# The per-layer embedding's projection issued in one piece ahead of the sum of squares

## The reference

```python
def rms_norm(x, g):
    xf = x.astype(jnp.float32)
    y = xf * lax.rsqrt(jnp.mean(xf * xf, axis=-1, keepdims=True) + EPS)
    return (y * g.astype(jnp.float32)).astype(x.dtype)

def per_layer_embed(h, p_i, g, w_gate, w_proj):
    gate = jax.nn.sigmoid((rms_norm(h, g) @ w_gate).astype(jnp.float32))
    return h + (gate * (p_i @ w_proj).astype(jnp.float32)).astype(h.dtype)

# first block
        x = x + moe(rmsnorm(x, g_ffn[i]), ...)
        gate = jax.nn.sigmoid(jnp.einsum('bsd,de->bse', rmsnorm(x, g_ple[i]), w_ple_gate[i]))
        x = x + jnp.einsum('bsp,pd->bsd', p[i], w_ple_proj[i]) * gate
# second block, for each of two layers
        h = h + peer_ffn(rms_norm(h, norm_ffn[i]), ...)
        h = per_layer_embed(h, p[i], norm_ple[i], ple_w_gate[i], ple_w_proj[i])
```

## Time and profile before

| | us |
|---|---|
| median of 3 runs | 3065.58 (3065.04 to 3068.65) |
| the profiled execution | 3064.01 |
| its span, first to last instruction | 3062.2 |
| TensorE busy | 2637.0 (86%) |
| VectorE busy | 1343.3 (44%) |
| mean granted clock of TensorE | 0.937 |
| first, second, third embedding: start of the projection | 1159.5, 2048.4, 3006.0 |

### The profile page before, as it was taken

One profiled execution on the slowest core, in us unless ns is written; L12 is line 12 of the kernel. 1 busy time (PEld: TensorE's weight loads), 2 busy tenths in 40 slices (PEclk: granted clock), 3 DMA queues, 4 the chain that ended last, 5 costly groups with the idle time before them and its releaser, 6 DMA issues.

```text
span 3062.2 us, 29257 instructions
## 1 busy us (share of the span) xinstructions
PE 2637.0 (86%) x10044; PEld 1391.2 (45%) x10044; DVE 1343.3 (44%) x3484; ACT 544.5 (18%) x1283; POOL 509.5 (17%) x556
## 2 busy tenths in 40 slices
PE   8789999999999998997778777789888778787787
PEld 6554444444443436784333333347677333333335
DVE  2222221212212223416777777641234777777752
ACT  0210010000101002202222222211331222122212
POOL 1000000000000000004333333300012333333320
PEclk9779999999999998998998999999889898989999
DMA  6259999999999993349999999953216999999990
GB/s 216 94 208 417 417 419 417 418 417 418 418 417 419 417 406 113 128 137 393 421 421 422 421 421 421 421 231 123 90 61 256 422 421 421 422 421 422 421 420 34
DMA packets 169837, 1025.92 MB, mean 335 GB/s; under 512 B 17488, under 2 KB 17904, under 8 KB 71184
## 3 DMA queue, kind: packets, MB, share of 16 engines
q0 software_dynamic: 74880, 540.05, 42.5%
q1 hardware_dynamic: 94864, 484.73, 40.1%
HBM read 1022.09 MB, written 2.62 MB: 335 GB/s over the span
## 4 chain that ended last, share of the span: by engine, by line
PE 44%; DMA 36%; DVE 8%; SPq 7%; issue 2%; ACT 2%; POOL 1%; DVEq 0%; ACTq 0%; POOLq 0%
DMA big<-in_uv,small 28%; PE ps L424 12%; PE ps L569 11%; PE ps L739 9%; DMA big<-in_w_gate_up 7%; SPq L342 4%; PE ps L559 3%; SPq L334 2%; PE ps L604 1%; DVE big L1477 1%; PE ps L414 1%; PE ps L437 1%; POOL big L1587 1%; PE ps L683 1%; DMA big<-in_w_down 1%
## 5 line engine op out<-in xcount | busy, mean ns | idle before, releaser
L739 PE MATMUL ps<-big,small 128*128 128x512 f32 x2048 | 1008.1, 650 | 283.8 <-ACT small L1039 283.8
L1587 POOL DMA_INDIRECT big<-in_uv,small x512 | 484.1, 946 | 2174.4 <-DVE small L1466 1406.6
L739 PEld LDWEIGHTS ps<-big,small 128*128 128x128 f32 x2048 | 415.2, 208 | 872.7 <-issue 492.9
L1477 DVE SCALAR_TENSOR_TENSOR big<-big,ps 128x1024 f32<-128x1024 f32 x512 | 617.6, 1219 | 349.6 <-DMA big<-in_uv,small 347.9
L569 PE MATMUL ps<-big 128*64 128x512 f32 x3072 | 705.8, 600 | 24.2 <-DMA big<-in_w_gate_up 21.6
L569 PEld LDWEIGHTS ps<-big 128*64 128x64 f32 x3072 | 202.9, 137 | 421.6 <-issue 333.9
L424 PE MATMUL ps<-hT,ring 128*128 128x256 f32 x1408 | 317.4, 388 | 14.5 <-DVE hT L1126 11.5
L424 PEld LDWEIGHTS ps<-hT,ring 128*128 128x128 f32 x1408 | 272.9, 195 | 58.6 <-DVE hT L1126 13.1
L1039 ACT ACTIVATE small<-con,small 128x128 f32<-128x128 f32 x512 | 163.6, 390 | 293.1 <-DVE small L1484 293.1
L1303 DVE COPY big<-ps 128x512 f32<-128x512 f32 x32 | 22.1, 692 | 426.1 <-PE ps L569 426.1
L1289 DVE TENSOR_TENSOR big<-ps,big 128x256 f32<-128x256 f32 x64 | 27.2, 425 | 308.2 <-PE ps L586 308.2
(11 more groups left out here) (246 smaller groups left out, 1633.2 us busy)
## 6 DMA issues: line engine op xcount, KB each, us to landing
big<-in_w_gate_up SPq DMA_DIRECT2D x256, 1024.0 KB, 20.5
big<-in_w_down SPq DMA_DIRECT2D x128, 1024.0 KB, 24.2
ring<-in_peer_w_q SPq DMA_DIRECT2D x32, 512.0 KB, 3.7
ring<-in_w_in SPq DMA_DIRECT2D x16, 512.0 KB, 5.2
ring<-in_a_w_in SPq DMA_DIRECT2D x16, 512.0 KB, 3.6
ring<-in_ple_w_gate SPq DMA_DIRECT2D x16, 512.0 KB, 5.9
big<-in_uv,small POOLq DMA_INDIRECT x512, 26.3
ring<-in_w_kv SPq DMA_DIRECT2D x16, 512.0 KB, 3.7
```

The costliest lines, as they stand in the source:

```text
L739: last = pe.matmul(ps[:, out_bank(tt) + z, :], diagonal(k), rows(k)[:, D + z * BANK:D + (z + 1) * BANK], start=(k % (PH * PTOP) == 0), sto ...
L1477: ins = dve.scalar_tensor_tensor(u, u, 1.0, tok, op0=ALU.mult, op1=ALU.mult, accum_out=dots[:, k:k + 1])
L1587: pool.indirect_dma_start(out=rows(k), out_offset=None, in_=io[f"uv{L}"], in_offset=bass.IndirectOffsetOnAxis(ap=rows_at[:, k:k + 1], axis ...
```

## The change

The projection's two halves are issued one behind the other, and `sum_squares` follows them. The wait for the residual is moved behind the projection, directly ahead of `sum_squares`. It can't be dropped, since `sum_squares` writes bank 7, which VectorE reads while it adds. The projection's banks 0 to 3 are not read by the adds. The number of instructions stays the same on every engine, and only TensorE's order changes, in all three places.

```diff
             def ple(k, norm, reads):
 
-                pe.wait_ge(x_ready, 4 * (norm - 1) + 4)
                 n = first[f"proj{k}"]
                 pe.wait_ge(p_loaded, 16 * (k + 1))
                 for c in range(2):
@@ -683,8 +682,8 @@
                         last = pe.matmul(half(0, e), w[:, e * P:(e + 1) * P], tile(pT, c),
                                          start=(c == 0 and e % 2 == 0), stop=(c == 1), skip_group_check=True)
                     last.then_inc(w_used, 1)
-                    if c == 0:
-                        sum_squares(norm)
+                pe.wait_ge(x_ready, 4 * (norm - 1) + 4)
+                sum_squares(norm)
                 dense(first[f"ple{k}"], hsrc, 4, h_ready, DT * reads)
```

## The result

The changed kernel takes 3079.09 us (median of 10 executions, 3072.27 to 3086.68), the kernel before 3067.77 us (10 executions beside them, 3064.95 to 3072.42). The ratio is 1.0036, 95% interval 1.0025 to 1.0048: 11 us slower, 8 to 15 by the interval. The profiled execution took 3076.04 us with a span of 3074.2, against 3064.01 and 3062.2.

What follows compares the result with a forecast made beforehand. TensorE's own work was taken to set the time in all three places. Stage 1 at +3.15 + 1.65, stages 2 and 3 at +3.15 - 0.97 + 1.65 each, gave +12.4 on 3065.6: 3078.0 us, range 3071 to 3083.

Steps and rivals of the forecast that it cites:

- The uncovered norm: Sum of squares to gate product, each stage: without the half between, 3.46 + 6.60 replaces 6.91 us, +3.15 per stage.
- The earlier start: Second and third stage: the projection no longer waits for the residual add and starts 0.97 us earlier in each.
- No gain at the front of the first stage: Behind the experts: projection start taken as unchanged, 0 gain within bounds of 0 and 3.1 us, since TensorE itself was late.
- The clock: Gate products behind the new 2.9 us idle time: lower granted clock costs 1.65 us per stage, bounds 0 and 3.1.
- The slow start of the first stage's projection: First stage: the projection's first half runs at half clock, 6.48 us for 3.46, and stays so with the start unchanged.
- Nothing else: Waits for residual and squares, last gate-weight loads and adds beside the projection's PSUM banks: other things that move cost nothing.
- the front of the first stage: Rival: TensorE starts the first stage's projection at 1156.4, full clock; +6.3 us in all, 3071.9; chance 0.08.
- The clock holds: Rival: gaps open ahead of the gate products but the clock holds, or slow stretches vanish; +7.5 us, 3073.1; chance 0.08.
- not issued early: Rival: another wait, embedding or weights, holds the projection; 3 x 4.8 = +14.4 us, 3080.0; chance 0.04.

Runs made afterwards that it cites:

- fillers: Changed kernel with seven matmuls of constants between the sum of squares and the gate product, where TensorE stood idle; ratio 1.0026 to the kernel before.
- a quarter of the cover: Against the kernel before: twelve of sixteen projection matmuls ahead of the wait and the sum of squares, four behind it; ratio 1.0007.
- the sum first: Against the kernel before: wait and sum of squares first, then both halves of the projection; ratio 1.0003.
- the new order without branches: Changed kernel without the three further expert passes and the branches over them, on all engines; 3071.91 us in one execution.
- the last version: Kernel before with only the first half early, plus six matmuls of constants behind sums of squares 3, 4, 5, 7 and 8; 3054.80 us, ratio 0.9960.

## Why the prediction was right

It said 3078.0 us, and the median is 3079.09; as a difference, +12.4 against +11.3 between the medians and +12.0 between the profiled spans. The mechanism was right. That the time came out within 1.1 us is partly luck: the difference was 1.1 too high, and the base, taken from three executions, 2.2 too low (3065.6 against 3067.77). Point by point:

- **The uncovered norm, +3.15 per stage.** The mechanism was right: the product follows the start of the sum of squares at a fixed distance, as long as what stands between is shorter: 6.49 us with nothing, with fillers and with a quarter of the cover. I had 6.60 from the bare sequence elsewhere, where the root starts 3.76 us after the sum, against 3.65 here: 0.11 too much per stage. The sum waits there for its squares, and here it doesn't. A sum of squares that starts behind a wait takes 3.69 to 3.72 us in these profiles, one that follows another piece 3.62; with the sum first the root starts 3.73 us after it, in the same stage. That accounts for most of the 0.11.
- **The earlier start, -0.97 in two stages.** It was 1.13 (2.11 us from the transposes' start before, 0.98 after). I had counted from the modelled end of the last transposes, and the next matmul is issued before that end. I had also left out that the first half of the projection, behind its wait, held TensorE for 3.55 us and now takes 3.46. So 2.18 less 0.11, 0.16 and 0.10 makes the 1.81 per stage.
- **No gain at the front of the first stage.** Right: the front is 0.14 us shorter in the profile after, and what holds it hangs on the branches. The 0.56 us of "issue" in the chain pointed there, against 3.31 us of idle time which the profile put down to the add; but 0.09 us stands in its place in another profile of the same order, so the row could have misled. SyncE's 6.5 us was the firmer sign. The bound was misread by a little: the expert matmuls end at 1156.21, not 1156.4. The Trainium skill (Runtime: NRT & Kernel Launch, Instruction fetch mechanics) names taken branches as a cause of stalls; the runs agree, with 2.7 us or more gone when the branches are.
- **The clock, 1.65 per stage.** 1.67, 1.67 and 1.70 were measured, and the choice of the nearest rows was what made it right: those with an unbroken run ahead. In most profiles that price comes back, but it is no fixed one, and that it came three times of three is partly luck. Behind an uncovered wait in one of the three embeddings, nine products in four kernels show 0.81 to 0.84 over their first 9 us eight times, and 0.65 once (3.1 us lost, in the third stage of the new order without branches, with just such an unbroken run ahead). Behind norm 8, one of the rows that I took, it is 0.81 to 0.83, 0.66 or 1.00, by the profile. So the prediction was right to allow anything between 0 and 3.1 from one run to the next, and the reason that it gave for its choice, the unbroken run, doesn't decide it.
- **The slow start of the first stage's projection, unchanged.** It was so in the profile after (9.95 us for both halves against 6.48 + 3.46), but 1.3 us less in two other kernels with the new order. That the profiled pair agrees is luck.
- **Nothing else.** The adds kept 1.29 and 2.48 us; the last gate loads were issued at 2057.00 and 3.78 us on, and no product waited for them.

The sum of the first two terms was 7.5 and is 6.5; the clock term 4.95 and 5.0. The remainder between the spans, 0.4, I had not put in the sum, only in the range, and its parts reach 1.9. Of the rivals the front of the first stage had the most behind it: without the branches the stage would have been 6.2 us shorter, which is what I had given for it (6.15). "The clock holds" is excluded by three windows, "not issued early" by the timeline.

## What to carry to other kernels

Work that depends on nothing is a filler, and a kernel has only so much of it: put it where the engine would wait longest and not where it could first be issued. Here one half of the projection can cover 1.1 us ahead of the sum of squares, and the other covers 2.9 behind it; moving both ahead gave the larger gap away. An idle time of TensorE's can cost twice, by its length and by the clock of what follows; read the windows behind such waits, and where nothing useful is left to fill them, even matmuls of constants can pay. And where a wait's releaser was done well before the engine starts, look at what its instruction stream does there: a moved wait doesn't help against branches.

## What the runs showed of the hardware

- Nested branches over three expert passes that aren't executed, with the use of a loaded count, cost TensorE 2.7 to 3.5 us, while it had the data for its next matmul (4.6 to 5.4 us from the mix to the projection in six profiles, 1.93 in the one without them).
- An idle time of 2.87 us behind an unbroken run of 10 us or more of matmuls lowered the clock to 1.2 GHz in each of the three places in the changed kernel (0.50 from 1176.2 to 1178 us, 1.00 from 1180 on), for 1.7 us of lost work each; one of 1.15 us lowered it in none of three. What lies between was not tried.
- Over all places the same wait had no fixed price. In the ten profiles other than that of the last version, 49 products stand behind 2.87 to 2.96 us of idle time, four or more in each (norms 4, 5, 7, 8 and the uncovered embeddings). Over their first 9 us 37 show clock 0.81 to 0.84, seven 0.65 to 0.67 and five 1.00, and the products behind norms 7 and 8 go through all three from profile to profile. The first product of the kernel (about 16 us), behind 3.02 us of idle time, shows 1.00 in seven of these profiles and 0.83 or 0.84 in three.
- Executions of the kernel before spread by 0.2 to 0.6% within a comparison (3058 to 3078 us across all of them), those of the kernel changed in the first place by 1.1%, more than many a change is worth. The same first stage, in the old order, took 18.70 us in one profile and 16.94 in another, as its projection fell on more or less of a slow stretch (6.65 and 5.37 us). Differences of 1 or 2 us are read from the stages, not from the medians.
